# Attention on one Trainium2 core: softmax shares put on in the matmul that turns the probabilities, by a diagonal tile, instead of by scaling before a transpose

## The chip, the cores and the metric

The kernel runs on one core of a Trainium2 chip. The metric is the time of one launch on the device in microseconds (us), the median of the runs. All data is f32.

## The reference, cut to what matters

A four-layer model on 256 latent tokens (the first two layers with 256 context tokens beside them), width 1024. Three of its layers hold softmax attention with heads of 64:

```python
def _softmax_attend(q, k, v):                       # first layer, 8 query heads, 2 key heads
    s = jnp.einsum('bhgqd,bhkd->bhgqk', q, k, preferred_element_type=jnp.float32) * (ATT_HEAD_DIM ** -0.5)
    p = jax.nn.softmax(s, axis=-1).astype(v.dtype)
    return jnp.einsum('bhgqk,bhkd->bhgqd', p, v)
...
    # third and fourth layer, 16 query heads, 4 key heads: causal, and sliding window with a sink
    m = jnp.maximum(jnp.max(logits, axis=-1, keepdims=True), sink)
    e = jnp.exp(logits - m)
    probs = e / (jnp.sum(e, axis=-1, keepdims=True) + jnp.exp(sink - m))
    out = jnp.einsum('bnkgqj,bnjkd->bnqkgd', probs.astype(v.dtype), vv)
```

The rest is projections, gated linear recurrences, feed-forward layers and a mixture of experts.

## The kernel before, in words

The program is a sequence of stages written for the engines by hand, each with its own semaphores and a meeting of four engines (`meet`) at its end. Attention is the function `attend`, called three times: for the first layer (two key heads, four tiles of 128 tokens; the two context tiles see two key tiles, the two latent tiles see four), and for the third and fourth layer (four key heads, two tiles of 128 tokens that see one and two key tiles, with a mask; the last of them with sinks too).

The work is cut into units: a key head `kv`, a query tile `qi` and a pair `p` of query heads. Each call has 16 units. A unit goes through these steps, all in one order written out by hand:

- TensorE, `scores`: two matmuls (one for each head of the pair) into `ps_s`, which has two buffers (L1078).
- VectorE, `maxima`: the negative row maximum (L1170, a reduction; with a mask L1179, which adds the mask on the way; with sinks L1177 too).
- ScalarE, `softmax`: exp of both heads into `att_probs_buf`, with the row sums into `att_stat` (L1129).
- VectorE, `shares`: the reciprocal of the sums (L1195) and for each head a scaling of its probabilities in place (L1198).
- TensorE, `turned`: the probabilities, 128 x 128 at a time, transposed into `ps_att_t`, a single buffer in PSUM (L1088): heads times key tiles, so 2, 4 or 8 transposes a unit.
- ScalarE and VectorE, `take_turned`: each copies one head of it to SBUF (L1137, L1188).
- TensorE, `output`: per key tile and head a matmul of the values (stationary, 64 columns) with the turned probabilities (L1099). The two heads alternate between the two halves of the columns of the array.
- ScalarE, `take`: the result out of PSUM (L1143).

In step `i` of the loop TensorE runs scores(i), turned(i-2), output(i-3); VectorE maxima(i), shares(i-1), take_turned(i-2); ScalarE take_turned(i-2), softmax(i), take(i-3). The staging of the next key head (keys L1058 and L1162, queries L1065 and L1119) is set between the steps. A group of transposes waits for the shares of its unit and for both copies of the unit before it.

`ident` is a 128 x 128 identity in `const`. A line with the name of another tile and `const` is one that reads it.

Of the kernel before, what the change touches and what calls it, by code (L numbers as in the profile page):

```python
# [9 lines left out]
ALU = mybir.AluOpType  # L10
# [3 lines left out]
P = 128  # L14
# [120 lines left out]
def program(nc, a, out):  # L135
# [4 lines left out]
    def unique(name):  # L140

        uses[name] = uses.get(name, 0) + 1
        return name if uses[name] == 1 else f"{name}_{uses[name]}"

    def sb(cx, name, shape, dt=F32):
        return cx.enter_context(nc.sbuf_tensor(unique(name), shape, dt))

    def pb(cx, name, shape, dt=F32):
        return cx.enter_context(nc.psum_tensor(unique(name), shape, dt))
# [25 lines left out]
    ident = const[:, C_IDENT:C_IDENT + P]  # L175
# [575 lines left out]
    def gla_pairs(A, g, T):  # L751
# [255 lines left out]

    s_att = {n: signal(n, o) for n, o in (
        ("att_staged", "tensor"), ("att_q_ready", "scalar"), ("att_k_ready", "vector"), ("att_scores", "tensor"),
        ("att_max", "vector"), ("att_probs", "scalar"), ("att_shares", "vector"), ("att_turned", "tensor"),  # L1010
        ("att_T_ready_a", "scalar"), ("att_T_ready_v", "vector"), ("att_out", "tensor"), ("att_taken", "scalar"))}

    def attend(A, q_col, k_col, v_col, kv_heads, q_tiles, room_T, made, mask=None, sinks=None, scale=1.0):
# [17 lines left out]
        keys_of = lambda u: q_tiles[units[u][1]][1]  # L1031
        with ExitStack() as cx:
# [2 lines left out]
            kT = sb(cx, "att_kT", [P, kv_heads, nkt * P])  # L1035
            own_column = 0 if sinks is None else 1
            probs = sb(cx, "att_probs_buf", [P, 2, 2, nkt * P + own_column])
            masked = sb(cx, "att_masked", [P, 2, 2, nkt * P + own_column]) if mask is not None else None
            minus = sb(cx, "att_minus_sinks", [P, 4 * kv_heads]) if sinks is not None else None
            stat = sb(cx, "att_stat", [P, 4, 4, 2])  # L1040
            probsT = room_T(cx, nkt)
            ps_s = [pb(cx, f"ps_att_s{i}", [P, 2, 512]) for i in range(2)]
            ps_t = pb(cx, "ps_att_t", [P, 2, 4, P])
            ps_o = pb(cx, "ps_att_o", [P, 512])
            ps_q = pb(cx, "ps_att_q", [P, 512])
            S = s_att

            @block.tensor
            def _(pe):
# [30 lines left out]
                    mm.then_inc(S["att_scores"].handle, 1)  # L1080

                def turned(u):
                    pe.wait_ge(S["att_shares"].handle, S["att_shares"].at(u + 1))
                    pe.wait_ge(S["att_T_ready_a"].handle, S["att_T_ready_a"].at(u))
                    pe.wait_ge(S["att_T_ready_v"].handle, S["att_T_ready_v"].at(u))
                    for h in range(2):
                        for k in range(len(keys_of(u))):
                            mm = nc.tensor.transpose(ps_t[:, h, k, :], probs[:, u % 2, h, k * P:(k + 1) * P], ident)  # L1088
                    mm.then_inc(S["att_turned"].handle, 1)

                def output(u):
# [12 lines left out]
                for i in range(n + 3):  # L1104
                    if i < n:
                        for r in stands[i]:
                            stage(r)
                        scores(i)
                    if 2 <= i < n + 2:
                        turned(i - 2)  # L1110
                    if i >= 3:
                        output(i - 3)
# [45 lines left out]
            def _(dve):  # L1158
                def keys(r):
                    kv, kind, b = rounds[r]  # L1160
                    dve.wait_ge(S["att_staged"].handle, S["att_staged"].at(r + 1))
                    nc.vector.tensor_copy(kT[:, kv, :], ps_q[:, 0:nkt * P]).then_inc(S["att_k_ready"].handle, 1)  # L1162
# [21 lines left out]
                def take_turned(u):  # L1184
                    nk = len(keys_of(u))
                    dve.wait_ge(S["att_turned"].handle, S["att_turned"].at(u + 1))
                    dve.wait_ge(S["att_out"].handle, S["att_out"].at(u - 1))
                    nc.vector.tensor_copy(probsT[:, u % 2, 1, 0:nk, :], ps_t[:, 1, 0:nk, :])\  # L1188
                        .then_inc(S["att_T_ready_v"].handle, 1)

                def shares(u):
                    nk = len(keys_of(u)) * P
                    total, inverse = stat[:, u % 4, 1, :], stat[:, u % 4, 2, :]
                    dve.wait_ge(S["att_probs"].handle, S["att_probs"].at(u + 1))
                    link_v(nc.vector.reciprocal(inverse, total))  # L1195
                    for h in range(2):
                        mine = probs[:, u % 2, h, 0:nk]
                        last = nc.vector.tensor_scalar(mine, mine, stat[:, u % 4, 2, h:h + 1], None, ALU.mult)  # L1198
                    last.then_inc(S["att_shares"].handle, 1)

                if sinks is not None:
                    link_v(nc.vector.tensor_scalar(minus[:, :], sinks[:, 0:4 * kv_heads], -1.0, None, ALU.mult))
                for i in range(n + 2):
                    if i < n:
                        for r in stands[i]:
                            if rounds[r][1] == "k":
                                keys(r)
                        maxima(i)
                    if 1 <= i <= n:
                        shares(i - 1)  # L1210
                    if i >= 2:
                        take_turned(i - 2)
            for k in ("att_scores", "att_max", "att_probs", "att_shares", "att_turned", "att_T_ready_a", "att_T_ready_v",
                      "att_out", "att_taken"):
                S[k].passed(n)
            S["att_staged"].passed(len(rounds))
# [2074 lines left out]
```

## Time and profile before

| | |
|---|---|
| median of 3 runs | 3291.54 us (3284.14 to 3292.17) |
| profiled execution, own time | 3291.54 us |
| its span, first to last instruction | 3289.7 us |
| mean granted TensorE clock | 0.969 |
| first attention, first to last transpose group | 247.68 to 284.98 us |
| second attention, the same | 1713.51 to 1742.18 us |
| third attention, the same | 2180.05 to 2210.17 us |

PE is TensorE's matmuls, PEld its weight loads, DVE VectorE, ACT ScalarE. Times of rows are us from the span's start unless marked ns. A granted clock of 1.00 is 2.4 GHz, 0.50 is 1.2 GHz. The length of a group of matmuls in a timeline contains the tail of its last one, so the start of the next group tells the pace.

### The profile page before, as it was taken

How to read it: one execution, taken by the hardware profiler on the slowest of the kernel's cores; microseconds unless marked ns; L12 is line 12 of the kernel's file. 1: busy time of each engine (PE TensorE's matmuls, PEld its weight loads, DVE VectorE, ACT ScalarE, POOL GpSimd, SP SyncE). 2: the span in 40 equal slices, each digit the busy share in tenths (PEclk: the TensorE clock that was granted, in tenths of full speed). 3: DMA queues.
4: the chain of work that ended last, by engine and by line, in shares of the span. 5: the costliest groups of instructions: out<-in, count | busy, mean ns of one | idle time of the engine just before them, and what ended most of it. 6: DMA issues, size and time to landing. Idle time of an engine off the chain costs nothing.

```text
span 3289.7 us, 41186 instructions
## 1 busy us (share of the span) xinstructions
PE 3069.8 (93%) x17936; PEld 1732.7 (53%) x17936; DVE 808.3 (25%) x1629; ACT 412.2 (13%) x1012; POOL 332.4 (10%) x376
## 2 busy tenths in 40 slices
PE   6988789999989999989998999988999999999998
PEld 2455544444447777667655777454434434444443
DVE  1138932000034766610033000243000000000002
ACT  1014111000022222110022000130000000000001
POOL 1123610000001333310000000000000000000030
PEclk9989988999999999989989999998999999999998
DMA  8670001312112222142443334226899999999992
GB/s 347 254 277 2 1 1 64 115 64 101 46 45 67 55 56 76 59 171 112 154 166 116 134 134 159 106 77 255 340 395 371 357 382 386 357 361 406 359 380 101
DMA packets 210611, 609.11 MB, mean 185 GB/s; under 512 B 6076, under 2 KB 53404, under 8 KB 203904
## 3 DMA queue, kind: packets, MB, share of 16 engines
q1 hardware_dynamic: 204912, 592.20, 47.3%
q0 software_dynamic: 5056, 13.67, 1.2%
q8 instruction: 144, 2.36, 0.3%
q10 hardware_dynamic: 464, 0.60, 0.1%
q14 instruction: 35, 0.29, 0.0%
HBM read 600.28 MB, written 6.16 MB: 184 GB/s over the span
## 4 chain that ended last, share of the span: by engine, by line
PE 83%; DVE 10%; issue 3%; ACT 2%; DMA 2%; POOL 1%; POOLq 0%; ACTq 0%; DVEq 0%
PE ps_ffn_gate L610 10%; PE ps_ffn_up L610 10%; PE ps_ffn_down L646 10%; PE ps_moe_down L3019 6%; PE ps_moe_gate L2974 6%; PE ps_moe_up L2974 6%; PE ps_odd L1928 4%; PE ps_lin L1408 4%; PE ps_project L528 3%; PE ps_moe_down L3025 3%; PE ps_moe_up L2979 3%; PE ps_moe_gate L2979 3%; PE ps_lin L296 3%; PE ps_ple_gate L2601 2%; DVE rec_qd L2187 2%
## 5 line engine op out<-in xcount | busy, mean ns | idle before, releaser
L610 PE MATMUL ps_ffn_gate<-hT,ring_buf 128*128 128x256 f32 (+1 forms) x1152 | 342.9, 451 | 4.3 <-issue 2.3
L610 PE MATMUL ps_ffn_up<-hT,ring_buf 128*128 128x256 f32 (+1 forms) x1152 | 336.7, 445 | 1.3
L646 PE MATMUL ps_ffn_down<-ring_buf,ffn_hiddenT 128*128 128x512 f32 x752 | 325.9, 593 | 3.0 <-issue 3.0
L610 PEld LDWEIGHTS ps_ffn_gate<-hT,ring_buf 128*128 128x128 f32 x1152 | 221.4, 193 | 120.3 <-issue 99.1
L610 PEld LDWEIGHTS ps_ffn_up<-hT,ring_buf 128*128 128x128 f32 x1152 | 217.9, 190 | 110.3 <-issue 90.0
L1928 PE MATMUL ps_odd<-ring_buf,hT 128*128 128x256 f32 (+2 forms) x1024 | 236.1, 385 | 8.1 <-ACT hg_kT L2063 6.4
L646 PEld LDWEIGHTS ps_ffn_down<-ring_buf,ffn_hiddenT 128*128 128x128 f32 x752 | 141.7, 190 | 182.0 <-issue 181.9
L695 DVE TENSOR_TENSOR ffn_hiddenT<-ffn_silu_buf,ps_ffn_up 128x256 f32<-128x256 f32 (+1 forms) x72 | 36.2, 502 | 726.5 <-PE ps_ffn_up L610 726.5
L3151 DVE TENSOR_TENSOR moe_hidden_buf<-moe_silu_buf,ps_moe_up 128x768 f32<-128x768 f32 (+1 forms) x32 | 27.3, 854 | 747.1 <-PE ps_moe_up L2979 747.1
L1928 PEld LDWEIGHTS ps_odd<-ring_buf,hT 128*128 128x128 f32 x1024 | 173.7, 192 | 55.2 <-ACT hg_kT L2063 7.9
L2974 PE MATMUL ps_moe_up<-ring_buf,moe_xg_buf 128*64 128x512 f32 (+1 forms) x1024 | 199.5, 542 | 0.3 <-DMA ring_buf<-in_w_exp_up_dram 0.3
L3019 PE MATMUL ps_moe_down<-ring_buf,moe_hiddenT 128*64 128x512 f32 x768 | 170.1, 595 | 0.7 <-DMA ring_buf<-in_w_exp_down_dram 0.7
L2974 PE MATMUL ps_moe_gate<-moe_third,moe_xg_buf 128*64 128x512 f32 (+1 forms) x768 | 142.8, 524 | 0.0
L667 ACT ACTIVATE ffn_silu_buf<-ps_ffn_gate 128x256 f32<-128x256 f32 (+1 forms) x72 | 32.3, 449 | 842.2 <-PE ps_ffn_gate L610 842.2
L1408 PE MATMUL ps_lin<-ring_buf,hT 128*128 128x448 f32 (+1 forms) x384 | 133.7, 502 | 0.0
L2974 PEld LDWEIGHTS ps_moe_up<-ring_buf,moe_xg_buf 128*64 128x64 f32 x1024 | 70.6, 137 | 111.8 <-issue 103.1
L3088 ACT ACTIVATE moe_silu_buf<-ps_moe_gate 128x768 f32<-128x768 f32 (+1 forms) x32 | 23.4, 731 | 698.7 <-PE ps_moe_gate L2979 698.7
L3019 PEld LDWEIGHTS ps_moe_down<-ring_buf,moe_hiddenT 128*64 128x64 f32 x768 | 53.5, 137 | 103.7 <-issue 103.0
L1408 PEld LDWEIGHTS ps_lin<-ring_buf,hT 128*128 128x128 f32 x384 | 71.9, 192 | 63.5 <-issue 59.0
L2979 PE MATMUL ps_moe_up<-ring_buf,moe_xg_buf 128*32 128x256 f32 (+1 forms) x2048 | 103.5, 354 | 0.0
L2974 PEld LDWEIGHTS ps_moe_gate<-moe_third,moe_xg_buf 128*64 128x64 f32 x768 | 53.0, 137 | 81.9 <-issue 73.8
L3187 POOL DMA_INDIRECT ring_buf<-moe_rows,moe_where x4 | 3.9, 975 | 875.1 <-POOLq L3182 874.2
(508 smaller groups left out, 3456.0 us busy)
## 6 DMA issues: line engine op xcount, KB each, us to landing
ring_buf<-in_w_exp_up_dram SPq DMA_DIRECT2D x24, 4096.0 KB, 16.6
ring_buf<-in_w_exp_down_dram SPq DMA_DIRECT2D x24, 4096.0 KB, 16.1
moe_third<-in_w_exp_gate_dram SPq DMA_DIRECT2D x16, 4096.0 KB, 17.7
mod_pieces<-in_mod_w_dram SPq DMA_DIRECT2D x40, 1024.0 KB, 6.5
ring_buf<-in_w_exp_gate_dram SPq DMA_DIRECT2D x8, 4096.0 KB, 17.5
ring_buf<-in_odd_w_in_dram SPq DMA_DIRECT2D x40, 512.0 KB, 5.2
moe_third<-in_w_exp_gate_dram SPq DMA_DIRECT2D x8, 2048.0 KB, 10.8
ring_buf<-in_w_exp_up_dram SPq DMA_DIRECT2D x8, 2048.0 KB, 7.7
```

What stands on the lines that cost most here:

```text
L296: mm = nc.tensor.matmul(ps[n % 4][:, 0:hi - lo], hT[:, k, t * P:(t + 1) * P], view[:, k, o:o + hi - lo], start=k == 0, stop=k == parts - 1)
L528: mm = nc.tensor.matmul(ps_y[i % 2][:, h * 512:(h + 1) * 512], of(k, t), view[:, k, :], start=k == 0, stop=k == KD - 1)
L610: mm = nc.tensor.matmul(ps[:, 0:wide], view[:, k, i * P:(i + 1) * P], hT[:, k, first_col:first_col + wide], start=k == 0, stop=k == KD - 1)
L646: mm = nc.tensor.matmul(ps_y[i % 2][:, h, :], hidT[:, b, i * P:(i + 1) * P], view[:, b, h * 512:(h + 1) * 512], start=first, stop=end)
L1408: mm = nc.tensor.matmul(ps_lin[:, n % 4, 0:hi - lo], hT[:, k, t * P:(t + 1) * P], view[:, k, o:o + hi - lo], start=k == 0, stop=k == KD - 1)
L1928: mm = nc.tensor.matmul(ps[:, 0:width], hT[:, k, t * P:(t + 1) * P], view[:, k, 0:width], start=k == 0, stop=k == KD - 1)
L2187: last = nc.vector.tensor_tensor(in_blocks(qd[:, d, l - 1, :], x), in_blocks(qd[:, d, l, :], x), query_factors(d, x), ALU.mult)
L2601: mm = nc.tensor.matmul(ps_gate[i][:, cols], hT[:, k, t * P:(t + 1) * P], view[:, k, :], start=k == 0, stop=k == KD - 1)
L2974: nc.tensor.matmul(ps[j * 64:(j + 1) * 64, 0:half], xg[:, k, 0:WIDE], w[:, k, j * half:(j + 1) * half], start=k == 0, stop=k == KD - 1, ti ...
L2979: mm = nc.tensor.matmul(ps[j * 32:(j + 1) * 32, half:half + quarter], xg[:, k, WIDE:ROOM], w[:, k, j * quarter:(j + 1) * quarter], start=k ...
L3019: nc.tensor.matmul(ps_y[j * 64:(j + 1) * 64, 0:512], x, w[:, b, j * 512:(j + 1) * 512], start=c == 0 and b == 0, stop=c == NP - 1 and b == ...
L3025: mm = nc.tensor.matmul(ps_y[j * 32:(j + 1) * 32, 512:768], x, w[:, b, j * 256:(j + 1) * 256], start=c == 0 and b == 0, stop=c == NP - 1 a ...
```

## The change

The probabilities are no longer scaled. VectorE writes for each head a 128 x 128 diagonal tile, the identity scaled row by row with the reciprocal of the sums, into a new buffer `att_diag_buf` (two units deep). TensorE no longer transposes but runs plain matmuls with the probabilities as the stationary tile and the diagonal as the moving one, which gives the transposed and scaled probabilities. It waits for the probabilities and for the diagonal by separate semaphores.

```diff
-        ("att_max", "vector"), ("att_probs", "scalar"), ("att_shares", "vector"), ("att_turned", "tensor"),
+        ("att_max", "vector"), ("att_probs", "scalar"), ("att_diag", "vector"), ("att_turned", "tensor"),
...
             probs = sb(cx, "att_probs_buf", [P, 2, 2, nkt * P + own_column])
+            diag = sb(cx, "att_diag_buf", [P, 2, 2, P])
...
                 def turned(u):
-                    pe.wait_ge(S["att_shares"].handle, S["att_shares"].at(u + 1))
+                    pe.wait_ge(S["att_probs"].handle, S["att_probs"].at(u + 1))
+                    pe.wait_ge(S["att_diag"].handle, S["att_diag"].at(u + 1))
                     pe.wait_ge(S["att_T_ready_a"].handle, S["att_T_ready_a"].at(u))
                     pe.wait_ge(S["att_T_ready_v"].handle, S["att_T_ready_v"].at(u))
                     for h in range(2):
                         for k in range(len(keys_of(u))):
-                            mm = nc.tensor.transpose(ps_t[:, h, k, :], probs[:, u % 2, h, k * P:(k + 1) * P], ident)
+                            mm = nc.tensor.matmul(ps_t[:, h, k, :], probs[:, u % 2, h, k * P:(k + 1) * P], diag[:, u % 2, h, :],
+                                                  start=True, stop=True)
                     mm.then_inc(S["att_turned"].handle, 1)
...
-                def shares(u):
-                    nk = len(keys_of(u)) * P
+                def diagonal(u):
                     total, inverse = stat[:, u % 4, 1, :], stat[:, u % 4, 2, :]
                     dve.wait_ge(S["att_probs"].handle, S["att_probs"].at(u + 1))
                     link_v(nc.vector.reciprocal(inverse, total))
                     for h in range(2):
-                        mine = probs[:, u % 2, h, 0:nk]
-                        last = nc.vector.tensor_scalar(mine, mine, stat[:, u % 4, 2, h:h + 1], None, ALU.mult)
-                    last.then_inc(S["att_shares"].handle, 1)
+                        last = nc.vector.tensor_scalar(diag[:, u % 2, h, :], ident, stat[:, u % 4, 2, h:h + 1], None, ALU.mult)
+                    last.then_inc(S["att_diag"].handle, 1)
...
                     if 1 <= i <= n:
-                        shares(i - 1)
+                        diagonal(i - 1)
```

## Rows read from the trace of the kernel before

**Rows 1.** The page: engines, and the chain that ended last, by engine.
```profile
PE 3069.8 (93%) x17936; PEld 1732.7 (53%) x17936; DVE 808.3 (25%) x1629; ACT 412.2 (13%) x1012; POOL 332.4 (10%) x376
...
PE 83%; DVE 10%; issue 3%; ACT 2%; DMA 2%; POOL 1%; POOLq 0%; ACTq 0%; DVEq 0%
```
**Rows 2.** Groups by line and form; busy us, mean ns of one, idle before.
```profile
L1088 PE MATMUL ps_att_t<-const,att_probs_buf 128*128 128x128 f32 x192 | 32.7, 295 | 8.7 <-DVE att_probsT L1188 6.1 <-DVE hT L1188 1.9 <-DVE att_probs_buf L1198 0.4
...
L1198 DVE TENSOR_SCALAR att_probs_buf<-att_probs_buf,att_stat 128x256 f32<-128x256 f32 x48 | 15.2, 358 | 0.9
L1099 PE MATMUL ps_att_o<-hT,even_A 128*64 128x128 f32 x192 | 14.0, 281 | 0.5 <-ACT even_A L1143 0.5
...
L1198 DVE TENSOR_SCALAR att_probs_buf<-att_probs_buf,att_stat 128x128 f32<-128x128 f32 x32 | 7.7, 284 | 0.6
...
L1198 DVE TENSOR_SCALAR att_probs_buf<-att_probs_buf,att_stat 128x512 f32<-128x512 f32 x16 | 7.1, 484 | 0.3
```
**Rows 3.** Windows: length, each engine's busy us and instructions, clock, DMA.
```profile
247.68:284.98 37.30, 35.23 (x304) 22.18 (x305) 33.07 (x74) 26.84 (x86) 0.54 (x1) 1.00 0.02 4
1713.51:1722.72 9.21, 9.21 (x59) 5.72 (x58) 6.56 (x33) 5.83 (x24) 0.00 (x0) 0.66 0.31 125
1722.72:1730.46 7.74, 7.11 (x65) 4.56 (x66) 6.48 (x34) 6.12 (x25) 0.00 (x0) 1.00 0.01 2
1730.46:1737.36 6.90, 6.20 (x53) 3.73 (x54) 6.05 (x33) 5.64 (x24) 0.00 (x0) 1.00 0.01 2
1737.36:1742.18 4.82, 3.38 (x29) 1.87 (x29) 4.31 (x20) 3.68 (x14) 0.00 (x0) 1.00 0.01 2
2180.05:2189.88 9.83, 9.65 (x60) 6.03 (x58) 7.41 (x39) 5.92 (x25) 0.00 (x0) 0.63 0.00 1
2189.88:2197.88 8.00, 7.11 (x66) 4.56 (x65) 7.09 (x39) 6.17 (x25) 0.00 (x0) 1.00 0.01 3
2197.88:2205.15 7.27, 6.13 (x54) 3.70 (x52) 6.66 (x38) 5.69 (x24) 0.00 (x0) 1.00 0.00 0
2205.15:2210.17 5.02, 3.32 (x29) 1.81 (x28) 4.53 (x22) 3.73 (x15) 0.00 (x0) 1.00 0.00 0
```
**Rows 4.** Chain of waits, first attention: start, us, engine, tile, line.
```profile
259.43 1.23 DVE att_stat L1170
...
261.16 0.48 DVE att_probs_buf L1198
...
262.39 1.06 PE ps_att_t L1088 x8
263.45 1.02 PE ps_att_o L1099 x16
264.48 0.63 PE ps_att_s L1078 x4
265.11 1.02 PE ps_att_t L1088 x8
```
**Rows 5.** Timeline, first attention, its first scaling pair and transpose group.
```profile
246.66 0.97 DVE L1198 TENSOR_SCALAR att_probs_buf<-att_probs_buf,att_stat 128x256 f32<-128x256 f32 x2
...
247.68 0.66 PE L1088 MATMUL ps_att_t<-const,att_probs_buf 128*128 128x128 f32 x4 [0.44 <-DVE att_probs_buf L1198]
```
**Rows 6.** Timeline of TensorE, recurrence of the second layer: plain matmuls.
```profile
1042.55 1.50 PE L1951 MATMUL ps_odd<-rec_qd,ring_buf 128*128 128x128 f32 x12
1043.88 0.39 PE L1951 MATMUL ps_odd<-rec_qd,hg_kT 128*128 128x128 f32 x2
```
**Rows 7.** Groups by form, TensorE's weight loads, 1032 to 1045 us.
```profile
L1951 PEld LDWEIGHTS ps_odd<-rec_qd,ring_buf 128*128 128x128 f32 x36 | 4.3, 192 | 1.3 <-DVE rec_qd L2187 1.3
```
**Rows 8.** Timeline, drain of the second attention.
```profile
1740.79 0.63 PE L1088 MATMUL ps_att_t<-const,att_probs_buf 128*128 128x128 f32 x4 [0.79 <-DVE att_probsT L1188]
...
1741.61 0.42 DVE L1188 COPY att_probsT<-ps_att_t 128x256 f32<-128x256 f32 x1
...
1742.18 0.63 PE L1088 MATMUL ps_att_t<-const,att_probs_buf 128*128 128x128 f32 x4 [0.39 <-DVE att_probsT L1188]
```
**Rows 9.** Chain of waits, second attention: an issue step.
```profile
1707.71 0.04 issue
```

More of the change, by code:

```diff
@@ L1209, in _ @@
                     if 1 <= i <= n:
-                        shares(i - 1)
+                        diagonal(i - 1)
                     if i >= 2:
                         take_turned(i - 2)
-            for k in ("att_scores", "att_max", "att_probs", "att_shares", "att_turned", "att_T_ready_a", "att_T_ready_v",
+            for k in ("att_scores", "att_max", "att_probs", "att_diag", "att_turned", "att_T_ready_a", "att_T_ready_v",
                       "att_out", "att_taken"):
```

## The prediction

> **What bounds the kernel now.** I read the page first. TensorE is busy for most of the span and 83% of the chain that ended last is its work [rows 1]. That is an average, so the question is who ends the waits inside the three calls of `attend`, the only place the diff touches. The view by line and form shows how often the changed lines run: 192 transposes on L1088 and 96 scalings on L1198, of three widths [rows 2].
>
> Next, windows over each call, cut where the pattern of one key head repeats [rows 3]. The reader is to compare TensorE's busy time with the length of each stretch. In the first layer, from the first transpose group to the last, it is 35.23 of 37.30 us, so 2.07 us are idle, while VectorE is busy 33.07. In the masked calls the first stretch has next to no idle time (0.00 and 0.18 us); the two middle ones have 0.63 and 0.70 us in the first masked call, 0.89 and 1.14 us in the second; only the last, the drain, has over 1.4 us. So attention is bound by TensorE with VectorE close behind. The chain of waits says the same: it passes from score matmuls to VectorE and back for some units, and in others it is TensorE step after step [rows 4]. What was removed from VectorE is therefore worth little, and what is put on TensorE has only those idle gaps to hide in.
>
> **The TensorE edit: 192 transposes become 192 plain matmuls.** First, how the trace counts: a transpose leaves one record (192 key-tile and head pairs, 192 records). A plain f32 matmul leaves two: the output loop of the first layer issues 96 and shows 192 [rows 2]. Price of a transpose: eight of them take 1.02 us until the next group begins [rows 4]; between a group of eight (1.06) and one of four (0.66) lie 0.40 us, 0.10 each [rows 4, 5]. I take 0.11 with the latency that a short group shows. Price of a plain 128x128x128 f32 matmul at the full clock: in the recurrence of the second layer 12 records of such matmuls start at 1042.55 and the next group at 1043.88, 1.33/12 = 0.111 us a record, 0.222 a matmul [rows 6]. Its operands are of the same shape, with a fresh stationary tile for each, as in the changed line. So each of the 192 costs 0.111 us more: 0.44 us for a unit of two key tiles, 0.89 for one of four, 0.22 for one of one.
>
> Bounds of that price: below, next to nothing extra, if the two records ran at the pitch of the output loop (16 records in 1.02 us, 0.064 each and 0.13 a matmul [rows 4]); but those alternate between two halves of the columns of the array, and the changed matmuls fill all of it. Above, 0.192 us a record if the weight load (192 ns [rows 7]) were not overlapped with the matmul before: +0.27 a matmul, +52 us. The rows with the same shape have that load and still run at 0.111 [rows 6], so I take 0.111 and don't let the range reach to either end.
>
> The Trainium skill, "TensorE: Matmul & The Clock Gate", section "Terms", calls the transpose mode four times faster for FP32. By that rule the plain matmul would cost 0.44 us against 0.11 and the 192 together some 63 us more. The pitch in rows 4 and 6 makes it a factor of two, so the sum goes by two.
>
> **The VectorE edit.** A pair of scalings of 256 columns becomes one of 128. Nearest rows: a 128-column scaling takes 284 ns, 256 columns 358, 512 columns 484 (means); narrowed, the last two lose 0.07 and 0.20 us each, 0.14 and 0.40 a pair [rows 2]. The new one reads `ident` and writes another buffer instead of in place, which no row shows; below it would cost 0.28 as here, above 0.36, which would cancel the gain for two key tiles. Over all: 8 pairs from 512 and 24 from 256 give 8 x 0.40 + 24 x 0.14 = 6.6 us of VectorE work. None for the 16 pairs of 128. It counts only where VectorE sets the pace.
>
> **Waits.** `turned` now waits for `att_probs` and `att_diag` separately. The diagonal is made only after `att_probs`, so the first has always come when the second does; behind them on TensorE's queue stand the matmuls of that unit and the output of the one before, whose semaphores are unchanged. ScalarE's order and `att_turned` are as before, only later by the longer group. The reciprocal stays. I cost this at nothing: one more semaphore already reached, 48 times, and where a group follows another TensorE group directly the queue is read ahead under the matmuls before it. If that cover were gone, 48 waits would cost at most some 2 us, an estimate with the 0.04 us of an issue step in the chain [rows 9] for each; it goes into the range only.
>
> **The sum, call by call.** New length of a stretch = TensorE's busy time + what is added, if that is more than VectorE's busy time, which it is everywhere (VectorE at most 33.07 against 45.0, and 7.09 against 8.44).
>
> First layer: before the last group stand 8 groups of four transposes and 7 of eight, 88 in all: 88 x 0.111 = 9.8. 35.2 + 9.8 - 37.3 = +7.7. The last group adds 0.9. The first begins when the first scaling pair is done, which took 0.97 us there, and waits 0.44 us for it [rows 5]; a narrower pair gives back about 0.3. Together +8.3.
>
> First masked call: the stretch from the first transpose group to the fifth has 14 of the matmuls and no idle time, +1.55 (its mean granted clock is 0.66, so some 6.3 of its 9.21 us ran at 0.50, the 1.2 GHz level, and the rest at 2.4 GHz; I assume that the clock returns at the same moment, so that work pushed behind it costs its full-clock time). The next two have 12 each [rows 3]: 7.11 + 1.33 - 7.74 = +0.70 and 6.20 + 1.33 - 6.90 = +0.63. In the drain the chain is a group, VectorE's copy of it, the next group: the 14th group is covered by the 0.79 us that TensorE idles before the 15th, which starts at 1740.79, and the last starts at 1742.18 [rows 8]. With 0.63 + 0.44 us for the 15th, tail and all, then the copy's 0.42 and 0.2 for two handoffs, the last starts at 1742.5, 0.3 later, and is 0.44 longer: +0.8. Together +3.7.
>
> Second masked call: 9.65 + 1.55 - 9.83 = +1.4, then 7.11 + 1.33 - 8.00 = +0.4 and 6.13 + 1.33 - 7.27 = +0.2, drain +0.8: +2.8.
>
> Sum +14.8. The profiled execution took 3291.54 us (span 3289.7 and 1.8 around it), which is also the median of the three, so I forecast 3306.3 us, +0.45%. Uncovered afterwards: after `attend` comes a meeting of all engines, so what is late there makes everything behind it late.
>
> **The rivals.**
>
> *All of it is exposed.* If handoffs stay between TensorE and VectorE (every group still waits for the single transposed bank), none of the idle is regained and all 192 count: 21.3 us, with the cold stretches at double price (the first three groups of either masked call, 16 matmuls, +1.8) 23.1 us: 3314.6. For it: groups wait for VectorE's copy of the group before [rows 8]. Against: with the group itself longer, the output and the next scores on TensorE (1.02 + 0.63 us [rows 4]) cover that copy. 20%.
>
> *VectorE is the bound, and the change is faster.* Nothing of TensorE's extra shows. Where the chain runs through VectorE [rows 4], narrower scalings shorten it: up to 6.6 us off, 3285. It decides only where VectorE's work per stretch stays above TensorE's after the change. In the second masked call (7.09 against 7.11) the two stand level now; it needs the addition of 1.33 us a stretch to be under the idle, and only the third stretch (1.14) comes near. 3%.
>
> *The clock comes back sooner.* In the first stretch of the masked calls 6.3 and 7.3 us run at 0.50 (0.66 of 9.21 and 0.63 of 9.83 us [rows 3]); twice the work on TensorE in those groups might bring the clock back sooner. At best all 13.6 us run at the full clock: 6.8 us back, +8.0 in all, 3299.5. Against it: in those stretches TensorE has hardly any idle time already (0.00 and 0.18 us) and the clock stays down all the same [rows 3]. The Trainium skill says on the same page, "Part 4: PE-mode transpose", that transposes do not count as busy for the clock gate, which would favour this rival; in the first layer's stretch the clock stays at 1.00 although 88 of its transposes, 0.13 us each and so a third of the time, are among the work [rows 3], which doesn't bear it out. 12%.
>
> **How the numbers follow.** Forecast 65%, rivals 20, 3 and 12. The forecast's own range is +10 to +18: low if the drain and the second masked call hide more, high if a third of the idle stays. The asked range has to take in the two likelier rivals in part: +7 to +23, 3298 to 3315. 0.3% (9.9 us) is about what a measurement of this kernel tells from no change; the three runs lie 8 us apart. Within it fall the clock rival, the VectorE rival and the bottom of the forecast (3%): 0.17 with a rounding up for the first; faster by more needs over 9.9 us where at most 6.6 are to be had: 0.01; slower 0.82.
>
> **What would show it.** the changed line with 384 records of 0.11 us pitch and weight loads of 192 ns; scalings of 96 at 128 columns; the first-layer stretch 45 us long with TensorE busy nearly all of it and the idle before its groups gone; VectorE now waiting for transposed banks. Wrong it would be if the records came at another pitch, if a wait on `att_diag` stood before groups, or if the clock row differed in the masked calls.

## The result, and the profile after

The changed kernel takes 3308.03 us (median of 4, 3306.90 to 3311.27), against 3290.38 us (median of 4) for the kernel before: ratio 1.0061, interval 1.0049 to 1.0074, which is +16 to +24 us. Run again beside other kernels it gave 3310.55 us (median of 5) against 3290.39, ratio 1.0057, 1.0043 to 1.0071. The forecast was 3306.3. Its sum of +14.8 us lies a little below both: the direction and the mechanism in attention held, and some 4 us came from a place that the forecast didn't look at.

The page of the changed kernel, its first line and the busy times (answers to [rows 1]):

```profile
span 3305.2 us, 41618 instructions
...
PE 3089.6 (93%) x18128; PEld 1757.4 (53%) x18128; DVE 802.9 (24%) x1629; ACT 411.6 (12%) x1012; POOL 333.7 (10%) x376
```

TensorE has 192 matmul records more and is busy 19.8 us longer; VectorE is busy 5.4 us less. The program has 432 instructions more than before (41186); that figure comes back below.

The groups by line and form (busy us, mean ns of one, idle time before), answering to [rows 2]:

```profile
L1090 PE MATMUL ps_att_t<-att_diag_buf,att_probs_buf 128*128 128x128 f32 x384 | 56.7, 292 | 5.2 <-DVE att_probsT L1191 4.4 <-issue 0.4
...
L1090 PEld LDWEIGHTS ps_att_t<-att_diag_buf,att_probs_buf 128*128 128x128 f32 x384 | 47.8, 196 | 22.4 <-issue 18.2 <-ACT att_probs_buf L1132 3.4
...
L1199 DVE TENSOR_SCALAR att_diag_buf<-const,att_stat 128x128 f32<-128x128 f32 x96 | 23.4, 286 | 1.7
```

The 384 records are there, with weight loads of 196 ns, and the 96 scalings are all 128 columns wide and take 286 ns each. The three lines of scalings before came to 30.0 us [rows 2]; 23.4 are left. The idle time ahead of the changed line went from 8.7 to 5.2 us.

Windows over the same stretches as [rows 3] (length; busy us and count of PE, PEld, DVE, ACT, POOL; granted clock; DMA share and GB/s): the first layer, first to last turning group but for a fraction of a microsecond, then the first three stretches of the first masked call, then those of the second masked call.

```profile
248.75:294.28 45.53, 45.53 (x393) 33.56 (x393) 29.75 (x74) 26.74 (x88) 0.46 (x1) 1.00 0.02 3
1722.12:1732.75 10.63, 10.63 (x71) 7.77 (x69) 6.46 (x33) 5.75 (x24) 0.00 (x0) 0.72 0.26 104
1732.75:1741.62 8.87, 8.54 (x78) 6.26 (x77) 6.40 (x33) 5.97 (x26) 0.00 (x0) 1.00 0.01 2
1741.62:1749.50 7.88, 7.55 (x67) 5.43 (x65) 5.98 (x32) 5.42 (x25) 0.00 (x0) 1.00 0.01 2
2190.71:2199.50 8.79, 8.01 (x69) 5.86 (x69) 7.05 (x37) 6.52 (x27) 0.00 (x0) 1.00 0.01 3
2199.50:2208.60 9.10, 8.61 (x79) 6.29 (x77) 7.07 (x37) 6.17 (x26) 0.00 (x0) 1.00 0.00 1
2208.60:2216.60 8.00, 7.52 (x67) 5.36 (x65) 6.64 (x36) 5.50 (x25) 0.00 (x0) 1.00 0.01 2
```

In the first layer TensorE is busy all of 45.53 us: the 2.07 us of idle time are gone. In the masked calls some stays: 0.33 us in each of the middle stretches of the first (0.63 and 0.70 before), 0.49 and 0.48 in the second (0.89 and 1.14 before).

The chain of waits in the first layer is now TensorE alone from 248.75 us on; three steps of key tiles two wide, three of four:

```profile
256.42 1.09 PE ps_att_t L1090 x8
257.50 0.59 PE ps_att_o L1102 x8
258.09 1.06 PE ps_att_s L1079 x4
...
264.76 1.02 PE ps_att_o L1102 x16
265.79 0.63 PE ps_att_s L1079 x4
266.42 1.98 PE ps_att_t L1090 x16
```

A group of four now lasts 1.09 us and one of eight 1.98.

**Where the time went, in the two profiled executions** (3307.04 and 3291.54 us, spans 3305.2 and 3289.7: +15.5). I take each call from the first matmul of its staging (`ps_att_q`) to the first matmul of the next stage: the first call went from 53.6 to 62.8 us (+9.2), the first masked one from 38.6 to 43.3 (+4.7), the second masked one from 40.8 to 40.6 (−0.2, but at another clock, below). That is 13.7. Late in the launch, after the experts' loop, 3.8 us more are lost at one place that the change doesn't touch; the stretches between give back 2.0. For that place, the timeline of TensorE before the scatter of the experts' result, first in the kernel before:

```profile
3225.95 1.93 PE L3025 MATMUL ps_moe_down<-moe_third,moe_hiddenT 128*32 128x256 f32 x32
3230.24 2.25 PE L3047 MATMUL ps_moe_down<-moe_ye,moe_back_buf 96*128 96x512 f32 x4 [2.36 <-DVE moe_ye L3166]
...
3240.78 1.97 PE L2509 MATMUL ps_turned<-const,Y 128*128 128x128 f32 x8 [5.15 <-DVE Y L2469]
```

and in the changed one:

```profile
3237.91 1.93 PE L3026 MATMUL ps_moe_down<-moe_third,moe_hiddenT 128*32 128x256 f32 x32
3244.99 3.77 PE L3048 MATMUL ps_moe_down<-moe_ye,moe_back_buf 96*128 96x512 f32 x4 [5.15 <-issue]
...
3256.53 1.97 PE L2510 MATMUL ps_turned<-const,Y 128*128 128x128 f32 x8 [5.15 <-DVE Y L2470]
```

The reader is to look at the brackets. Before, TensorE waited 2.36 us for VectorE's copy. After, it is idle for 5.15 us and nothing that the profile shows releases it ("issue"). From the first of these rows to the last it is 14.83 us before and 18.62 after. I call this the scatter stretch.

### The profile page after: what moved, and what is told of

It reads as the page before. It is cut to its first block, busy times and chain, and to the rows that moved or that the text cites. A ratio compares the mean times of both kernels' runs of the same rounds, so it can differ in the third digit from the quotient of the medians.

```text
span 3305.2 us, 41618 instructions
## 1 busy us (share of the span) xinstructions
PE 3089.6 (93%) x18128; PEld 1757.4 (53%) x18128; DVE 802.9 (24%) x1629; ACT 411.6 (12%) x1012; POOL 333.7 (10%) x376
## 4 chain that ended last, share of the span: by engine, by line
PE 84%; DVE 9%; issue 3%; DMA 2%; ACT 2%; POOL 1%; POOLq 0%; ACTq 0%; DVEq 0%
PE ps_ffn_gate L610 10%; PE ps_ffn_up L610 10%; PE ps_ffn_down L646 10%; PE ps_moe_down L3020 6%; PE ps_moe_gate L2975 6%; PE ps_moe_up L2975 6%; PE ps_odd L1929 4%; PE ps_lin L1409 4%; PE ps_project L528 3%; PE ps_moe_down L3026 3%; PE ps_moe_up L2980 3%; PE ps_moe_gate L2980 3%; PE ps_lin L296 3%; PE ps_ple_gate L2602 2%; DVE rec_qd L2188 2%
## 5 line engine op out<-in xcount | busy, mean ns | idle before, releaser
L3089 ACT ACTIVATE moe_silu_buf<-ps_moe_gate 128x768 f32<-128x768 f32 (+1 forms) x32 | 23.4, 731 | 698.8 <-PE ps_moe_gate L2980 698.8
```

## The experiments

### The matmul edit alone

From the kernel before (arguments shortened):

```diff
-    mm = nc.tensor.transpose(ps_t[:, h, k, :], probs[...], ident)
+    mm = nc.tensor.matmul(ps_t[:, h, k, :], probs[...], ident, start=True, stop=True)
```

The scalings on VectorE and the one wait on `att_shares` stay as they were.

> TensorE's part of the change alone: plain matmuls against the identity in place of the transposes, the scaling by VectorE kept as it was. If the cost is TensorE's 0.11 us more a matmul with VectorE already off the bound, the time is that of the changed kernel, +16 to +19 us over before, and the groups last 1.09 us (four) and 1.98 us (eight). Rival, VectorE's shorter work is what holds the changed kernel's loss down: up to 6.6 us more than the changed kernel, +22 to +25.

Measured: 3304.37 us (5 runs), ratio 1.0049, 1.0035 to 1.0063. The first call takes 62.9 us, as in the full change (62.8), the masked ones 43.6 and 41.0 (43.3 and 40.6 there). The matmul edit alone makes the whole loss in attention. The idle time before the scatter is short, 2.13 us, and the scatter stretch takes 14.61 us in place of 18.62, which is about what this kernel lies under the changed one.

### The diagonal alone

This run starts from the changed kernel. VectorE makes the diagonal, and TensorE transposes the probabilities with `ident` as before, so the shares are left out of the output: the result isn't scaled.

> VectorE's part alone: the diagonal is written, but TensorE still transposes by the identity, so the shares are left out of the result (the probabilities stay unscaled). If TensorE is the bound with VectorE close behind, only its idle gaps can close: -1 to -4 us. Rival, VectorE bounds attention: the whole 6.6 us of its work, -5 to -7. Rival, the pair of narrow scalings is hidden everywhere: 0.

Measured: 3410.47 us (5 runs), ratio 1.0373, which says nothing of the edit. The page shows why: the experts' loop runs more often. A row of its matmuls, first of the kernel before, then of this one:

```profile
L2974 PE MATMUL ps_moe_gate<-moe_third,moe_xg_buf 128*64 128x512 f32 x512 | 113.4, 595 | 0.0
```

```profile
L2974 PE MATMUL ps_moe_gate<-moe_third,moe_xg_buf 128*64 128x512 f32 x576 | 127.6, 595 | 0.0
```

Other values route the tokens otherwise, and the number of passes follows the data; the expectation had not thought of it. What can be read is the attention itself, ahead of that. Windows from the first to the last turning group of the first layer, here:

```profile
249.57:285.76 36.19, 35.09 (x307) 22.20 (x305) 29.27 (x74) 26.85 (x86) 0.00 (x0) 1.00 0.02 4
```

and in a second profile of the kernel before:

```profile
249.45:287.08 37.63, 35.39 (x305) 22.18 (x305) 33.10 (x74) 27.20 (x88) 0.32 (x1) 1.00 0.02 3
```

So the narrower scalings are worth 1.1 to 1.4 us in the first layer (36.19 against 37.30 [rows 3] and 37.63) as long as TensorE has idle time; next to the plain matmuls they are worth 0.1 (62.8 against 62.9 us a call).

### By place: the first layer alone, the masked calls alone

```diff
+    if mask is None:         # the first layer; the other run has "mask is not None"
         ...                  # the changed form, on TensorE and on VectorE
+    else:
+        ...                  # the form of before
```

> The whole change in the first attention only, both masked calls as before. By the forecast's sum +8.3 us; by the trace of the changed kernel, whose first attention is 9.2 us longer, +9. Rival, the recurrence behind it takes back the 2 us that it lost in offset in that trace: +7.

Measured: 3298.77 us (7 runs), ratio 1.0025, 1.0013 to 1.0036, or +8.2; the first call takes 63.2 us.

> The whole change in the two masked calls only. By the forecast's sum +3.7 and +2.8, together +6.5. By the trace of the changed kernel +4.7 in the second attention and -0.2 in the third, where the granted clock was 1.00 throughout and before it was 0.50 for the first 14 us. If that clock was luck, the two calls come out +8 to +10 when the clock falls in both traces and the time is +7 to +9. Rival, plain matmuls keep the clock up in the third call: the clock row is 1.00 there again and the time is +4 to +5.

Measured: 3295.40 us (11 runs), ratio 1.0021, 1.0011 to 1.0030, or +6.9. The masked calls take 43.3 and 41.7 us. The two ratios add up to +15 us, near the forecast's +14.8. The full change has +19 to +20. In both of these runs the scatter waits only 2.13 us, and the scatter stretch takes 14.61 and 12.91 us; in the full change it is 18.62 and 18.81 (second profile), 3.8 to 4.0 us longer than in the kernel before. That place is about the difference. The intervals of the two ratios leave some 4 us on their sum open, so this comparison alone would not prove it.

### The same two kernels again, on one chip

> The kernel before once more, for its clock rows. If the granted clock of the third attention is chance, it may come out as 1.00 this time; if it goes with the transposes, it is 0.50 for the first 4 us or more again. Time 3284 to 3293.

> The changed kernel once more, against the kernel before on this chip. Forecast +14.8 us; the two halves of the change run alone gave +8.2 and +6.9, so +15 to +17. First attention 62.8 us from its first staging to the next stage, second 43.3. Third 40.6 if plain matmuls keep the clock up there, about 44 with the clock at 0.50 for the first 14 us if the clock of that call is chance.

Measured: 3290.73 us for the kernel before (one run), 3310.55 (5 runs) for the changed one. The first call takes 53.8 and 63.5 us (+9.7), the first masked one 38.2 and 42.1 (+3.8). The second masked call of the kernel before now takes 37.0 us with 28.43 from the first to the last turning group, in place of 40.8 and 30.12:

```profile
2181.48:2209.91 28.43, 23.19 (x200) 14.36 (x201) 25.48 (x132) 22.19 (x90) 0.00 (x0) 1.00 0.00 1
```

Its clock is 1.00 throughout, with transposes. (In the first profile it was 0.83 over the call.) The changed kernel shows the opposite pair: 1.00 throughout in its first profile (40.6 us) and 0.88 over the call in the second (43.6 us). So either kernel can have that call with the clock down at its start or not. At the full clock it is 37.0 against 40.6, +3.5; with it down 40.8 against 43.6, +2.8.

### Each plain matmul twice

```diff
-    mm = nc.tensor.matmul(ps_t[:, h, k, :], probs[...], diag[:, u % 2, h, :], start=True, stop=True)
+    for _ in range(2):
+        mm = nc.tensor.matmul(ps_t[:, h, k, :], probs[...], diag[:, u % 2, h, :], start=True, stop=True)
```

> The changed kernel with each of the 192 plain matmuls issued twice. If a plain f32 matmul costs 0.222 us of TensorE wherever it stands and TensorE is the bound throughout, the time is that of the changed kernel plus 42.6 us, so before +57 to +60; groups of 16 and 32 records last 1.98 and 3.75 us. Rival, idle of TensorE still takes some of it in the masked calls: +53 to +56.

Measured: 3347.49 us (4 runs), ratio 1.0176, 1.0161 to 1.0192, or +53 to +63 us against the kernel before and 36.9 over the changed one on the same chip, 0.19 us for each of the 192. The expectation's 42.6 did not come in full. Call by call, against the first profile of the changed kernel, the first call is 22.2 us longer, more than the 21.3 that 96 matmuls cost, the masked ones 6.7 and 8.7, where 48 matmuls cost 10.7. In the third attention, where the clock is 1.00 in both, 2 us of them thus ran in time in which TensorE would have idled; in the second the clock was down for a shorter time in this run, so that 6.7 can't be taken as a price. The chain of waits gives the price directly:

```profile
249.58 1.98 PE ps_att_t L1091 x16
...
263.52 3.77 PE ps_att_t L1091 x32
```

8 matmuls take 1.98 us, 16 take 3.77, and 4 took 1.09: (3.77 − 1.98)/8 = 0.224 and (1.98 − 1.09)/4 = 0.222 a matmul, and 0.2 us more that each group costs once. For transposes, in the chain of the kernel before, a group of eight takes 1.02 us [rows 4] and one of four:

```profile
267.79 0.59 PE ps_att_t L1088 x4
```

That is (1.02 − 0.59)/4 = 0.11 each and 0.16 a group.

### TensorE's separate wait for the probabilities taken out

The diagonal is made behind `att_probs`, so the wait for it covers both.

```diff
-    pe.wait_ge(S["att_probs"].handle, S["att_probs"].at(u + 1))
     pe.wait_ge(S["att_diag"].handle, S["att_diag"].at(u + 1))
```

> The changed kernel without TensorE's separate wait for the probabilities (the diagonal is made behind them), which takes 48 instructions out of TensorE's stream ahead of the expert layer and nothing else. Its stream is then as long as that of the run with plain matmuls and kept scalings. If the 3 us that TensorE idles longer before the last scatter of the experts (5.2 us in both traces of the changed kernel, 2.1 to 2.4 in five others) hang on where that code lies in the stream, the idle is 2.1 to 2.4 here and the time 3 us under the changed kernel, +15 to +17 over before. Rival, the waits cost time where they stand: attention shorter, idle before the scatter 5.2 as before. Rival, neither: +19.

Measured: 3301.98 us (6 runs), ratio 1.0034, 1.0022 to 1.0046. The first call is as long as before, its window too:

```profile
248.93:294.43 45.50, 45.50 (x395) 33.52 (x393) 29.86 (x74) 26.79 (x88) 0.34 (x1) 1.00 0.02 3
```

But the long idle time ahead of the scatter is gone, and the clock stays up behind it; the scatter stretch takes 12.91 us in place of 18.62:

```profile
3242.75 1.98 PE L3047 MATMUL ps_moe_down<-moe_ye,moe_back_buf 96*128 96x512 f32 x4 [2.13 <-DVE moe_ye L3166]
```

So 48 waits cost nothing where they stand, and their 48 instructions (41618 against 41570) cost 3 us of idle time some 1000 us after the last of them, in another stage, and 5.7 us with the clock that falls in it. It isn't the luck of one execution: the 21 executions of the changed kernel on record with its result took 3306.2 us or more, five of the six here 3303.6 or less.

### Instructions added to the kernel before: two misses

Between the long and the short kernels lay the number of instructions: the two runs of the changed kernel (432 more than before) and the doubled matmuls (1200 more) had the long idle time, those with 0, 240 and 384 more (and the run with a bank for each unit, below, with 64 fewer) the short one (the experts' loop runs equally often in all of them). 432 and 1200 are both 176 above a multiple of 256. The block of 256 is a guess: 432 and 1200 lie 768 apart, so these numbers fit any divisor of 768 as well that keeps the others out, such as 128 or 384. I added satisfied waits to TensorE's stream ahead of the first attention, to have 176 and 128 instructions more:

```diff
+    for _ in range(176 if nt == 4 else 0):     # 128 in the other run
+        pe.wait_ge(S["att_staged"].handle, S["att_staged"].at(0))
     for i in range(n + 3):
```

> The kernel before with 176 waits that are already met, on TensorE ahead of the first attention, where TensorE idles for 9.8 us. The changed kernel has 432 instructions more than before and the run with doubled matmuls 1200 more; both leave 176 over a multiple of 256, and both show the long idle. If the place in blocks of 256 instructions is what counts, the idle before the last scatter is 5.1 to 5.3 us and the time +3. Rival, the idle comes from something else in the change: 2.1 to 2.4 and 0 to +1.

> The same with 128 such waits, the remainder of the run with plain matmuls and kept scalings (384 more), which showed the short idle. Both theories: idle before the last scatter 2.1 to 2.4 us, time 0 to +1; a longer time would be the price of the waits themselves.

Measured: 3299.51 and 3294.74 us (12 runs each), ratios 1.0026 (1.0017 to 1.0035) and 1.0014 (1.0005 to 1.0024). Neither of the two theories of the first was tested. Two waits go into one instruction, so the program grew by 88 and 64 instructions (41274 and 41250), not by 176 and 128, and neither met the condition; the idle time stayed at 2.13 us in both. And the waits cost time themselves, so that both times lie above what was expected: the first attention began late, after 19.26 us without TensorE's work in place of 9.77 (16.69 with the 64). Before, that idle time ends with the meeting of the engines; the added waits stand behind the meeting in TensorE's program, so none of them can hide in it. That makes 9.49/88 and 6.92/64, both 0.108 us an instruction:

```profile
244.68 1.72 PE L1058 MATMUL ps_att_q<-const,even_A 128*64 128x128 f32 x13 [19.26 <-issue]
```

### 80 instructions more than the changed kernel

This is the test of place against number. If the place counts, a *longer* stream than that of the changed kernel should be rid of the idle time too. 160 waits make 80 instructions, 512 more than the kernel before, and they stand at the launch's start, where TensorE has nothing to do for 12 us.

```diff
+    for _ in range(160):
+        pe.wait_ge(S["cond_silu"].handle, S["cond_silu"].at(0))
     pe.wait_ge(S["cond_silu"].handle, S["cond_silu"].at(1))
```

> The changed kernel with 160 waits that are already satisfied, in TensorE's stream at the launch's start, where TensorE is idle for 12 us until its first operand comes. Two of them go into an instruction, so 80 instructions more than the changed kernel, 512 more than the kernel before. All earlier runs with 0, 64, 88, 240 or 384 instructions more than the kernel before had a short idle time ahead of the scatter at the end of the experts (2.1 to 2.4 us), those with 432 and 1200 (each 176 above a multiple of 256) a long one (5.2 to 5.3). Theory of place: what counts is where the instructions after the experts' loop fall in the blocks in which the stream is fetched, so 80 more bring the idle time back to 2.1 to 2.4 us, and the time to 3 us under the changed kernel's, about 3303 to 3305, although the stream is longer. Theory of length: a longer stream makes the idle time no shorter, it stays at 5.1 us or more, and the time is that of the changed kernel, 3307 to 3310. Both expect the first product at 12 us as before; if the waits took more than 0.15 us a pair they would push it out, and the total with it.

Measured: 3302.55 us (6 runs), ratio 1.0033, 1.0021 to 1.0045. The page and the timeline:

```profile
span 3305.9 us, 41698 instructions
```

```profile
3242.78 1.93 PE L3028 MATMUL ps_moe_down<-moe_third,moe_hiddenT 128*32 128x256 f32 x32
3246.85 3.08 PE L3050 MATMUL ps_moe_down<-moe_ye,moe_back_buf 96*128 96x512 f32 x4 [2.13 <-DVE moe_ye L3169]
...
3257.39 1.97 PE L2512 MATMUL ps_turned<-const,Y 128*128 128x128 f32 x8 [5.15 <-DVE Y L2472]
```

The idle time is 2.13 us and the stretch 14.61 in place of 18.62 us, and the median lies 5.5 and 8.0 us under the two of the changed kernel. A longer stream is rid of the idle time as a shorter one is, so it isn't the number of instructions that costs but where they come to lie. One part of the expectation missed: the waits didn't fit into the 12 us, the first product came at 16.02 us in place of 11.95 (0.2 us a pair); the next group waits for data and starts at 24.01 us, against 23.99 in the changed kernel. The profiled execution was the slowest of the six (3307.78 us): its first attention starts 1.8 us later than in the changed kernel's and the stage after it is 1.6 longer, which takes up most of the 4.0 us.

### A bank for each unit

The idle time that is left before transposes in the masked calls ends with VectorE's copy out of the single transposed buffer. This run goes at that instead, from the kernel before, with transposes and scalings kept: in the masked calls a unit needs at most half of the buffer, so units take its two banks in turn, and ScalarE alone copies both heads in one instruction.

```diff
+    small = 1 if nkt <= 2 else 0
...
-    pe.wait_ge(S["att_T_ready_a"].handle, S["att_T_ready_a"].at(u))
-    pe.wait_ge(S["att_T_ready_v"].handle, S["att_T_ready_v"].at(u))
+    pe.wait_ge(S["att_T_ready_a"].handle, S["att_T_ready_a"].at(u - small))
+    if not small:
+        pe.wait_ge(S["att_T_ready_v"].handle, S["att_T_ready_v"].at(u))
```

> The kernel before, with transposes and shares, but in the masked calls each unit has a PSUM bank of its own for its turned probabilities, two in turn, and ScalarE copies both heads, so VectorE copies none and a group no longer waits for the copy of the unit before. If that wait and VectorE's work are what TensorE idles for there (0.63 to 1.14 us a stretch and 1.4 to 1.7 in the drain), -3 to -6 us. Rival, the chain through ScalarE, which gets 0.2 us more a unit, takes its place: -1 to +2.

Measured: 3283.81 us (11 runs), ratio 0.9981, 0.9972 to 0.9990: faster than both kernels. The window of the first masked call, here and in the second profile of the kernel before:

```profile
1713.00:1739.22 26.22, 23.50 (x203) 14.48 (x201) 19.70 (x103) 23.08 (x87) 0.00 (x0) 1.00 0.12 48
```

```profile
1715.38:1742.58 27.20, 23.26 (x203) 14.39 (x201) 23.22 (x118) 21.33 (x87) 0.00 (x0) 1.00 0.13 49
```

TensorE's work is the same, its idle time goes from 3.94 to 2.72 us, and VectorE has 3.5 us less to do. The whole calls take 35.9 and 35.7 us against 38.2 and 37.0, so 3.7 us of the some 6 are seen there. Not all of that is the edit's. From the last transpose group on, the second attention takes 2.98 us here and 4.33 in the second profile of the kernel before, where the clock is down in that stretch, against 2.95 in its first profile, where it is up:

```profile
1742.58:1746.91 4.33, 3.26 (x21) 2.15 (x21) 0.42 (x1) 0.94 (x3) 0.00 (x0) 0.50 0.00 0
```

```profile
1739.22:1742.20 2.98, 1.91 (x21) 1.28 (x21) 0.00 (x0) 1.36 (x5) 0.00 (x0) 1.00 0.00 0
```

So the edit shows 1.0 us in the first masked call and 1.4 in the second, and 1.3 us are the clock. The scatter stretch is 12.92 us here and 14.83 in both profiles of the kernel before, again by the clock (last section): 1.9 us more. Of the some 6 us about 2.4 are what the edit does in attention, then, and 3.3 are clock in two places; whether these come with the edit or by chance, no run shows.

A transpose with the diagonal in the place of the identity wasn't tried. If it gave the scaled result, it would keep TensorE at the price of a transpose and VectorE at the narrow scalings.

## Why the prediction was right, step by step

**Bound by TensorE.** Right. In the first layer the chain is TensorE alone and the busy time is the whole stretch.

**The price of a plain matmul.** 0.222 us forecast, 0.222 and 0.224 measured; two records each, weight loads of 196 ns, overlapped. The Trainium skill, "TensorE: Matmul & The Clock Gate", section "Terms", calls the transpose mode four times faster for FP32. The measurement decides otherwise: the run with doubled matmuls and [rows 4] make it a factor of two (0.22 against 0.11). Too small by a little was the term of a whole group: I priced groups by 0.111 for each matmul alone, +0.44 and +0.89, and they came out 0.50 and 0.96 longer (1.09 − 0.59 and 1.98 − 1.02), 0.06 to 0.07 a group. The first call became 9.2 us longer and not 8.3: from first to last group it grew by 8.2 for my 7.7, behind that by 1.0 for my 0.9, and ahead of it by nothing (12.02 us from the call's start to the first group before, 12.07 after), where I had let the narrower first pair give 0.3 back. What the fixed part of a group (0.20 us for plain ones, 0.16 for transposes) consists of, no run tested.

**Idle time regained.** Right in the first layer (2.07 of 2.07 us), too hopeful in the masked calls: of their middle stretches' idle time 0.33, 0.33, 0.49 and 0.48 us stay, where I had let it all go. Stretch by stretch the first masked call gave +1.42, +1.13 and +0.98 for my +1.55, +0.70 and +0.63, and with the drain +4.7 for +3.7. In the second pair of profiles that call gave +3.8, but there the clock was down for different stretches in the two kernels, so the agreement is luck in part. The second masked call gave +2.8 for +2.8 between the two profiles that have the clock down at its start, as the forecast assumed, and +3.5 between the two that have it up. The mechanism of the rival "all of it is exposed" thus holds for a part: groups there still wait for VectorE's copy of the group before.

**The VectorE edit.** Right in both: 6.6 us less scaling work (30.0 to 23.4 us), 286 ns each although it reads another tile, and worth nothing for the time, since TensorE sets the pace. Alone it is worth 1.1 to 1.4 us in the first layer.

**The second wait.** I costed it at nothing with the reason that TensorE's queue is read ahead. For the place where it stands that is shown. What the step left out is that the 48 instructions shift all code behind them. The kernels with 432 and 1200 instructions more than the kernel before lost 3.8 to 4.0 us against it after the experts' loop, and those with another number (64 fewer, 0, 64, 88, 240, 384, 512 more) lost nothing there. Which places between these numbers cost time stays open. This is the larger part of what the sum lacked. In the run without that wait the medians are 6.1 and 8.6 us lower; 5.7 of that is the scatter stretch (18.62 against 12.91), 3.0 idle time and 2.7 clock, and in its profile the first masked call is 2.5 us shorter too, because the clock was down there for a shorter time.

**The rivals.** "All of it is exposed", 3314.6: no, see above. By the total alone it could not be told from the forecast: 3308.03 lies nearer the forecast, 3310.55 midway, and 4 us of both come from outside attention. The traces decide, where the idle time of the first layer is gone. "VectorE is the bound", 3285: no. "The clock comes back sooner", 3299.5: no. In the first stretch of the first masked call the granted clock rose from 0.66 to 0.72 on average because the stretch grew by work at the full clock: 6.3 of its 9.21 us were at the 1.2 GHz level before and 6.0 of 10.63 after. In the second masked call either kind of matmul is seen with the clock at 1.00 from start to end. The Trainium skill says in "TensorE: Matmul & The Clock Gate", section "Part 4: PE-mode transpose", that transposes don't count as busy for the clock. These runs don't bear it out: the clock in that call was down in the first profile of the kernel before and in the second of the changed one, and up in the other two. No run has transposes alone for a stretch, so they don't refute it either.

**The numbers.** The sum of the calls, with the sizes as measured: 9.2 + 4.7 + 3.5 = +17.4, with the scatter's 3.8 about +21, against +16 to +24. By the second pair of profiles it is 9.7 + 3.8 + 6.6 + 4.0 = +24 (the 6.6 and 4.0 below). In the profiled pair the stages between gave 2.0 us back, in the pair of second profiles 3.2; there the scatter stretch cost 4.0 us and the second masked call 6.6, with the clock down in one kernel and not in the other (43.6 against 37.0). What these stages do was not looked into.

## What to carry to other kernels

Where TensorE sets the pace, as in this kernel, don't move work from VectorE into the form of a matmul: an f32 transpose leaves one record and costs half of a plain matmul of its shape, and VectorE time saved is worth next to nothing there. Price groups by groups of the same size in the trace, not by the pitch within one. When the measured sum lacks a few microseconds, look for an idle time that ends with no releaser in a stage that nothing touched, and shift the stream by some instructions before you explain it by the change. And read the clock of a stretch in both profiles before you compare its length: here it made 3.7 us between two profiles of one call of one kernel (40.8 and 37.0).

## What the runs showed of the hardware

**Where the instructions lie can cost 4 us.** In the changed kernel TensorE stands still for 5.15 us after a loop whose length the data sets. During this time the weights' queue runs, and one packet of instructions moves. The queues in half a microsecond of it, 3241.91 to 3242.41 us (packets, MB, share of the DMA engines):

```profile
q1 hardware_dynamic: 92, 0.19, 102.3%
q8 instruction: 1, 0.02, 13.6%
```

Counted from the first of the loop's last matmuls (3237.91), that is 4.0 us, two after TensorE fell idle. In the second profile of the changed kernel the packet moves at 4.0 us too, in the run with doubled matmuls at 4.5, both with the long idle time. In no profile without it does a packet move between 1 and 7 us: the kernel before has them at 0 and 7.5, the others at 0 or at 10 to 12, or at both. That TensorE waits for this packet behind the weights is the reading that fits. That the packet is TensorE's, and that it is what ends the idle time, isn't shown: the profile names no releaser. What the runs show is that the place in the stream decides and the number of instructions doesn't, and that the idle time is 5.15 to 5.32 us in the three profiles of the two kernels that have it and 2.13 to 2.36 in all others.

**The clock falls in that idle time, and in some kernels soon after the short one.** The first four scatter matmuls took 3.77 us in both profiles of the changed kernel, 2.25 and 2.73 in those of the kernel before, 2.93 to 3.12 in three runs (the first layer alone, the matmul edit alone, 80 instructions more) and 1.98 in the others, the one without the second wait among them. Windows over them, in the changed kernel and in the one without that wait, have the clock in the third figure from the end, 0.50 (1.2 GHz) and 1.00 (2.4 GHz):

```profile
3245.00:3248.60 3.60, 3.60 (x5) 1.53 (x6) 0.00 (x0) 0.00 (x0) 0.00 (x0) 0.50 0.95 367
```

```profile
3242.70:3244.50 1.80, 1.75 (x4) 0.87 (x5) 0.00 (x0) 0.00 (x0) 0.00 (x0) 1.00 1.05 388
```

In the kernel before the clock falls during the scatter, here over all eight of its matmuls, so it pays for a part of this as well:

```profile
3230.24:3235.63 5.39, 5.39 (x8) 1.87 (x8) 1.22 (x1) 0.00 (x0) 0.00 (x0) 0.68 1.05 395
```

The scatter stretch thus has three lengths: 12.91 us with the clock up to the end of the scatter, 14.61 to 14.83 with a clock that falls in it, 18.62 and 18.81 with the long idle time. Against the kernel before, the changed one pays 2.8 us of idle time and 1.0 of clock, against the run without the second wait 3.0 and 2.7. What decides between the first two lengths was not looked into.

**Satisfied waits aren't free.** Two fit in one instruction (176 waits made the program 88 instructions longer, 128 made it 64). Behind a meeting such an instruction costs 0.108 us, at the launch's start 0.2: 80 of them put the first product at 16.02 us, 4 beyond the 12 that were free. The 48 in the changed kernel stand behind matmuls and cost nothing.
